# Seven quarter products in place of eight in differential attention's queries and keys and in a recurrent block's key and value halves

## The reference, cut

```python
def diff_attention(x, w_qkv, w_o, lam, subln_g, lambda_init):
    q, k, v = jnp.split(x @ w_qkv, 3, axis=-1)
    ...
    s = jnp.einsum('bqhcd,bkhd->bhcqk', q_blk, k) * scale
    p = jax.nn.softmax(jnp.where(causal, s, -jnp.inf), axis=-1)
    attn = p[:, :, 0] - lam_full * p[:, :, 1]
    ...
def rwkv7_time_mix(x, mu, w_rkv, ...):
    xx = jnp.pad(x, ((0, 0), (1, 0), (0, 0)))[:, :-1] - x
    xm = x[None] + xx[None] * mu[:, None, None, :]
    r, k, v = jnp.einsum('nbsd,nde->nbse', xm[:3], w_rkv)
    ...
```

## Time and profile before

| | us |
|---|---|
| median of 3 runs | 1956.05 (1954.45 to 1958.23) |
| profiled execution | 1958.03 |
| its span | 1956.2 |
| TensorE busy | 1647.6 (84% of the span) |
| VectorE busy | 679.4 (35%) |
| ScalarE busy | 370.8 (19%) |
| GpSimd busy | 195.0 (10%) |
| chain that ended last | TensorE 59%, transfers 32%, VectorE 5% |
| mean granted clock of TensorE | 0.93 |

### The profile page before, as it was taken

How to read it: one execution, slowest core, us unless ns; L and a number is a source line. 1 busy time by engine, 2 the same in 40 slices (tenths; PEclk the granted TensorE clock), 3 DMA queues, 4 the chain that set the end, 5 groups by cost and what they waited for, 6 DMA issues and landing times.

```text
span 1956.2 us, 29793 instructions
## 1 busy us (share of the span) xinstructions
PE 1647.6 (84%) x12826; PEld 1038.9 (53%) x12826; DVE 679.4 (35%) x1163; ACT 370.8 (19%) x748; POOL 195.0 (10%) x91
## 2 busy tenths in 40 slices
PE   9999999999999998776666797999988778676664
PEld 7998986997995854222122242867954223221211
DVE  1564431464541265211111124573365211111103
ACT  1444101343211251000000011331211000000001
POOL 2331422331330000000000000000300000000000
PEclk9999999999999999978887998999999989987877
DMA  9341444251355438999999998222156999999994
GB/s 384 103 169 52 186 181 164 85 167 72 151 204 204 172 135 351 427 427 428 427 427 427 425 419 341 106 86 67 68 238 285 426 428 426 426 426 427 427 427 194
DMA packets 48228, 537.10 MB, mean 275 GB/s; under 512 B 4533, under 2 KB 12981, under 8 KB 15033
## 3 DMA queue, kind: packets, MB, share of 16 engines
q1 hardware_dynamic: 46752, 528.27, 65.9%
q10 hardware_dynamic: 1304, 6.51, 0.8%
HBM read 533.71 MB, written 1.05 MB: 273 GB/s over the span
## 4 chain that ended last, share of the span: by engine, by line
PE 59%; DMA 32%; DVE 5%; ACT 2%; issue 1%; POOL 0%; ACTq 0%; DVEq 0%
PE ps L450 48%; DMA extra<-in_moe_w_gu 12%; DMA arena<-in_moe_w_gu 9%; PE ps L462 8%; DMA arena<-in_moe_w_down 6%; DMA ring<-in_moe_w_gu 4%; PE ps L468 2%; DVE x L1545 1%; DVE arena L1534 1%; ACT arena L2459 1%; ACT arena L2455 1%; DVE arena L1539 1%; DVE arena L1545 0%; ACT L2455 0%; DMA tcom<-in_tcom 0%
## 5 line engine op out<-in xcount | busy, mean ns | idle before, releaser
L462 PE MATMUL ps<-arena 128*32 128x512 f32 (+1 forms) x1348 | 204.4, 689 | 81.3 <-DMA arena<-in_moe_w_gu 65.0
L450 PE MATMUL ps<-hT,ring 128*128 128x256 f32 (+1 forms) x1472 | 262.5, 336 | 0.0
L2459 ACT ACTIVATE arena<-ps 128x512 f32<-128x512 f32 (+4 forms) x150 | 90.2, 601 | 879.0 <-PE ps L462 493.3
L462 PE MATMUL ps<-ring,arena 128*32 128x512 f32 x1248 | 181.9, 715 | 88.5 <-DMA ring<-in_moe_w_gu 69.7
L450 PEld LDWEIGHTS ps<-hT,ring 128*128 128x128 f32 x1472 | 233.4, 191 | 25.6 <-issue 2.1
L1534 DVE TENSOR_TENSOR arena<-arena,ps 128x256 f32<-128x256 f32 (+3 forms) x119 | 64.5, 542 | 511.6 <-ACT arena L2455 433.7
L462 PEld LDWEIGHTS ps<-arena 128*32 128x32 f32 (+1 forms) x1348 | 48.9, 126 | 220.2 <-DMA arena<-in_moe_w_gu 97.5
L450 PE MATMUL ps<-arena 64*64 64x64 f32 (+11 forms) x1456 | 142.4, 344 | 26.3 <-ACT arena L2748 22.3
L450 PE MATMUL ps<-arena,ring 64*64 64x64 f32 (+3 forms) x1344 | 146.9, 292 | 3.1 <-ACT hT L2459 1.4
L462 PEld LDWEIGHTS ps<-ring,arena 128*32 128x32 f32 x1248 | 38.0, 121 | 207.0 <-DMA ring<-in_moe_w_gu 101.1
L450 PEld LDWEIGHTS ps<-arena,ring 64*64 64x64 f32 (+2 forms) x1344 | 129.1, 161 | 18.3 <-DVE arena L1545 1.8
(11 more groups left out here) (204 smaller groups left out, 1820.3 us busy)
## 6 DMA issues: line engine op xcount, KB each, us to landing
arena<-in_moe_w_gu SPq DMA_DIRECT2D x57, 2048.0 KB, 41.3
ring<-in_moe_w_gu SPq DMA_DIRECT2D x49, 2048.0 KB, 41.3
ring<-in_moe_w_down SPq DMA_DIRECT2D x35, 2048.0 KB, 41.3
arena<-in_moe_w_down SPq DMA_DIRECT2D x29, 2048.0 KB, 40.6
extra<-in_moe_w_gu SPq DMA_DIRECT2D x22, 2048.0 KB, 40.8
ring<-in_w_merge SPq DMA_DIRECT2D x16, 2048.0 KB, 8.2
ring<-in_w_in SPq DMA_DIRECT2D x9, 2048.0 KB, 7.3
ring<-in_attn_w_qkv SPq DMA_DIRECT2D x6, 2048.0 KB, 7.2
```

Of the source, the lines that this page charges most:

```text
L450: i = t.matmul(o, l, r, start=first, stop=last, skip_group_check=True)
L462: i = t.matmul(o, l, r, start=first, stop=last, skip_group_check=True)
L2459: s.activation(o, a, ACT.Copy).then_inc(*act.one(name))
```

## The change

The products q0, k0, q1, k1 of attention and k1 and v1 of the recurrent block are made from seven quarter products each. With the weight half cut in quarters a (by depth and columns) and the input in quarters b (by depth and tokens), the parts are p1 = a11 b11, p6 = s2 h2, p7 = a21' h3 and p5 = s1 h1 into one PSUM tile ("a"), and p2 = a12 b21, p4 = a22 h4 and p3 = s4 b22 into a second ("b"). Each part is 8 matmuls with 128 columns (v1: 4 matmuls with 256). GpSimd makes a21' = a11 - a21 in place, s2 = a22 - a21', s1 = a11 + s2 and, when p6 is done, s4 = a12 - s2 over s2; the four input sums h are made once for attention and once each for k1 and v1. ScalarE copies p1's quarter, VectorE adds the others: four additions after p5 ("half": tile a is free), one after p2 and two after p3 ("out").

Scores wait for VectorE's "out" in place of ScalarE's copy. In attention the parts of q1 and k1 stand between the units where the column groups stood. VectorE makes q1's first additions after u0, its last after u1, k1's first after u2, its last after u3. The ring's slots of these products come free with part 3.

The diff, cut to its core. TensorE in attention:

```diff
-        def proj_qk(name, half, *cs):
-            n = f"da {name}{half}"
-            p = opened(n, cs[0] == 0, cs[-1] == 3, (act, n))
-            mm(proj_T(wcols(m.w(n), KT, 512), hT, KT, [(p[:, c * 256:(c + 1) * 256], slice(c * P, (c + 1) * P)) for c in cs]),
-               n if cs[-1] == 3 else None)
+        def proj_qk(name, half, *parts):
...
+                if q in (1, 2):
+                    tile(name2, *(((dve, n + " out"),) if late else ((act, n + " p1"), (dve, n + " half"))))
...
+                elif q == 6:
+                    t.wait_ge(*pool("da hsum"))
+                    t.wait_ge(*pool(n + " s2"))
+                elif q == 5:
+                    t.wait_ge(*pool(n + " s1"))
+                elif q == 3:
+                    t.wait_ge(*pool(n + " s4"))
+                mm([(p[:, 256 * i + P * e:256 * i + P * e + P], a[:, k, P * e:P * e + P], b[:, k, :], k == 0, k == 3)
+                    for e in range(2) for k in range(4)], f"{n} p{q}")
...
-            t.wait_ge(*act(f"da q{g // 2}"))
-            t.wait_ge(*act(f"da k{g // 2}"))
+            t.wait_ge(*dve(f"da q{g // 2} out"))
+            t.wait_ge(*dve(f"da k{g // 2} out"))
```

TensorE in the recurrent block (the inner `seven` gives out the parts 1, 6, 7, 5 and 2, 4, 3; ahead of 6 it waits for "hsum", ahead of 3 for "s4"):

```diff
-        proj("k", "rw mix1", r.xa, (1,))
+        seven("rw k1", r.xa, False)
...
+            if half:
+                seven(n, r.xc, True)
+                return
```

VectorE in attention; in the recurrent block it makes the same seven additions for "rw k1" ahead of `mix(0)` and for "rw v1" between `inverse_starts(0)` and `inverse_starts(1)`:

```diff
+        def first_sums(name, half):
...
+            v.wait_ge(*act(n + " p1"))
+            tt(c12, c11, area(p, 1), ADD)
+            v.wait_ge(*pe(n + " p5"))
+            tt(c21, c12, area(p, 2), ADD)
+            tt(c22, c21, area(p, 3), ADD)
+            tt(c12, c12, area(p, 3), ADD, n + " half")
+
+        def last_sums(name, half):
...
+            v.wait_ge(*pe(n + " p2"))
+            tt(c11, c11, area(p, 0), ADD)
+            v.wait_ge(*pe(n + " p3"))
+            tt(c21, c21, area(p, 2), ADD)
+            tt(c12, c12, area(p, 3), ADD, n + " out")
```

GpSimd in attention:

```diff
+    for c, name in enumerate(("q0", "k0", "q1", "k1")):
+        n, s2 = "da " + name, d.s2[c % 2]
+        (a11, a12), (a21, a22) = quarters(wcols(m.w(n), KT, 512))
+        g.wait_ge(*m.w.landed(n))
+        both(a21, a11, a21, SUB)
...
+        both(s2, a22, a21, SUB, n + " s2")
+        if c:
+            g.wait_ge(*pe("da " + ("q0", "k0", "q1")[c - 1] + " p5"))
+        both(s1, a11, s2, ADD, n + " s1")
...
+        g.wait_ge(*pe(n + " p6"))
+        both(s2, a12, s2, SUB, n + " s4")
```

GpSimd in the recurrent block:

```diff
+            for n, x, mixed, was in (("rw k1", m.rw.xa, "rw mix1", "moe0 end"), ("rw v1", m.rw.xc, "rw mix2", "rw k1 p3")):
...
+                g.wait_ge(*m.w.landed(n))
+                both(a21, a11, a21, SUB)
+                g.wait_ge(*pe(was))
+                both(s2, a22, a21, SUB)
+                both(s1, a11, s2, ADD)
+                g.wait_ge(*dve(mixed))
+                both(h3, b22, b12, SUB)
+                both(h1, b12, b11, SUB)
+                both(h2, b22, h1, SUB)
+                both(h4, b21, h2, SUB, n + " hsum")
+                g.wait_ge(*pe(n + " p6"))
+                both(s2, a12, s2, SUB, n + " s4")
```

More of the change, by code:

```diff
@@ L370, in memory @@
     d.S2, d.P2 = ([carve(512), carve(1024)] for _ in range(2))
+    d.hsum = [flat(m.mT)[:, 512 * i:512 * i + 512].rearrange("p (k s) -> p k s", k=4) for i in range(4)]
+    d.s2 = [carve(1024).rearrange("p (k n) -> p k n", k=4) for _ in range(2)]
+    at[0] = OWN - 1024
+    d.s1 = carve(1024).rearrange("p (k n) -> p k n", k=4)
     at[0] = 0
@@ L1257, in rwkv, with seven, part @@
                 for c in range(4)], "rw k0" if k == KT - 1 else None)
-        proj("k", "rw mix1", r.xa, (1,))
+        (h1, h2, h3, h4), (s1, s2) = m.hsum, m.wsum
+        def seven(n, x, turned):
+            (a11, a12), (a21, a22) = quarters(wcols(m.w(n), KT, 512))
+            (b11, b12), (b21, b22) = [[x[:, 4 * k:4 * k + 4, P * i:P * i + P] for i in range(NT)] for k in range(2)]
+            def part(p, i, a, b, q):
+                if turned:
+                    mm([(p[:, 256 * i:256 * i + 256], b[:, k, :], a[:, k, :], k == 0, k == 3) for k in range(4)], f"{n} p{q}")
+                else:
+                    mm([(p[:, 256 * i + P * c:256 * i + P * c + P], a[:, k, P * c:P * c + P], b[:, k, :], k == 0, k == 3)
+                        for c in range(2) for k in range(4)], f"{n} p{q}")
+            p = tile(n + " a", (act, n + " p1"), (dve, n + " half"))
+            t.wait_ge(*m.w.landed(n))
+            part(p, 0, a11, b11, 1)
+            t.wait_ge(*pool(n + " hsum"))
+            part(p, 1, s2, h2, 6)
+            part(p, 2, a21, h3, 7)
+            part(p, 3, s1, h1, 5)
+            p = tile(n + " b", (dve, n + " out"))
+            part(p, 0, a12, b21, 2)
+            part(p, 2, a22, h4, 4)
+            t.wait_ge(*pool(n + " s4"))
+            part(p, 3, s2, b22, 3)
+        seven("rw k1", r.xa, False)
         lv = wcols(m.w("rw lora1"), KT, 288)
@@ L1966, in oT_half @@
                MUL, None, n + " out b")
-        for n in range(4):
+        for name in "qk":
+            first_sums(name, 0)
+            last_sums(name, 0)
+        for n, more in enumerate((lambda: first_sums("q", 1), lambda: last_sums("q", 1), lambda: first_sums("k", 1), lambda: last_sums("k", 1))):
             front(*units[n])
             back(*units[n])
+            more()
         squares(1, 0)
@@ L2244, in rwkv, with seven @@
         mix(4, r.xc)
-        v.wait_ge(*pe("rw k1"))
+        def seven(n, c4):
+            (c11, c12), (c21, c22) = c4
+            p = ps(n + " a")
+            v.wait_ge(*act(n + " p1"))
+            tt(c12, c11, area_of(p, 1, c11), ADD)
+            v.wait_ge(*pe(n + " p5"))
+            tt(c21, c12, area_of(p, 2, c11), ADD)
+            tt(c22, c21, area_of(p, 3, c11), ADD)
+            tt(c12, c12, area_of(p, 3, c11), ADD, n + " half")
+            p = ps(n + " b")
+            v.wait_ge(*pe(n + " p2"))
+            tt(c11, c11, area_of(p, 0, c11), ADD)
+            v.wait_ge(*pe(n + " p3"))
+            tt(c21, c21, area_of(p, 2, c11), ADD)
+            tt(c12, c12, area_of(p, 3, c11), ADD, n + " out")
+        seven("rw k1", [[r.kT[:, 4 + 2 * j:6 + 2 * j, P * i:P * i + P] for i in range(NT)] for j in range(2)])
         mix(0, r.xa)
@@ L2332, in rwkv @@
             inverse_starts(i)
+            if i == 0:
+                seven("rw v1", [[r.vt[:, j, 512 + 256 * n:768 + 256 * n] for j in range(NT)] for n in range(2)])
         v.wait_ge(*pe("rw bonT"))
@@ L2871, in rwkv @@
                        bias=vcol(bias, 4 * half + c))
+        s.wait_ge(*dve("rw k1 out"))
         for k in range(KT):
@@ L2891, in rwkv @@
         s.wait_ge(*dve("rw pc"))
-        for half in range(2):
-            n = f"rw v{half}"
-            s.wait_ge(*pe(n))
-            cp(r.vt[:, :, 512 * half:512 * half + 512], ps(n).rearrange("p (t n) -> p t n", t=NT), n)
+        s.wait_ge(*pe("rw v0"))
+        cp(r.vt[:, :, 0:512], ps("rw v0").rearrange("p (t n) -> p t n", t=NT), "rw v0")
+        s.wait_ge(*pe("rw v1 p6"))
+        cp(r.vt[:, 0, 512:768], ps("rw v1 a")[:, 0:256], "rw v1 p1")
         def out(i, n, dst, mark=" out"):
```

73 lines of the change are left out of this document (56 added, 17 removed).

## The result

| | us |
|---|---|
| before, median of 7 runs | 1956.89 |
| after, median of 7 runs | 1963.96 (1960.01 to 1967.15) |
| ratio | 1.0038, interval 1.0028 to 1.0049 |
| after, once more (11 runs) | 1964.43, ratio 1.0034, interval 1.0019 to 1.0049 |
| forecast | 1962.5, range 1953 to 1968 |

The changed kernel is slower, by about 7 us. The profiled execution of after took 1967.15 with a span of 1965.1; it is the longest of its seven, so not all of its 9 us over the profile of before belong to the change. To keep chance apart I cut the span at four marks that every trace has: q0's first matmul, the issue of the next chunk into `extra` (765.00 in the earlier trace rows), the first transposes of the recurrent block, and the next issue into `extra` (1375.09 in the earlier trace rows). The stretches between them are called A (attention), M (the first experts) and R (the recurrent block).

The account below looks back on a forecast made before the run. TensorE's path in attention and the recurrent block was taken to set when expert-weight transfers start, and so the kernel's end. Attention +3.5 and recurrent block +3.0 gave +6.5 over the median 1956.05: 1962.5 us, range 1953 to 1968.

Parts of the forecast that it names:

- q0 and k0, -2.8: Attention's first two products: seven parts save 1.4 us of TensorE each, with GpSimd's sums and VectorE's additions costing nothing.
- The sums hold VectorE: GpSimd's sums and VectorE's two-input SBUF instructions wait for each other, as in the first layer; turn-taking given chance 0.58.
- taking turns, each waits for one sum: Attention, u0's two products: 2 x 2.43 plus 0.3 us, so the second ends at 671.25 in place of 666.09.
- Pauses in attention: TensorE idles 1.3 us ahead of the third score, 4.4 or 2.1 at u0's values, then 3.
- Attention +3.5: Differential attention: +2.7 us net of q0 and k0's gain, plus 0.8 for half clock; between +1.5 and +5.6.
- The second rival, no holding: GpSimd and VectorE don't hold each other: attention -3.6, in all -6.5 us, 1949.5; chance 0.17.
- the term for VectorE's additions: Second rival, attention: quarter adds of 1.85 us push u1 by 1.7, but TensorE has other parts to do meanwhile.
- k1, -0.8: Recurrent block: -1.4 us on TensorE, sums hold the first mix instructions about 1.2; net between -1.4 and +0.9.
- v1: Recurrent block: N0 idles 1.6 us, part 6 waits 3.0 for input sums until 1328.4; +2.9, up to +4.5.
- The mis-sized term: TensorE runs at half clock after a pause: 3.3 us so cost 1.65; v1 up to +4.5 with such a stretch.
- The sum: Whole kernel: attention +3.5 and recurrent block +3.0 make +6.5 us, 1962.5 against the median.
- A and R carry through to the end: Attention's end sets the expert transfers' start, likewise the recurrent block; each us won or lost reaches the kernel's end.

Follow-up runs that it names:

- the run with the sums cut short: Changed kernel with q1's fourth weight sum and all four of attention's k1 cut to one column; one execution, only attention read: A 135.59 us, against 139.15.
- the second trace of before: The kernel before, unchanged, profiled once more: A 136.62, M 453.15, R 157.64 us.
- the recurrent block alone: Seven parts in the recurrent block only, attention as in the kernel before: R 162.44 us, ratio 1.0023 to the kernel before, +4.5 us.
- v1 early: Changed kernel with v1's four input sums made before GpSimd waits for v1's weights: R 156.11 us, ratio 1.0011 to the kernel before, +2.2 us.
- q0 and k0 alone: Seven parts for q0 and k0 only, all else as in the kernel before: ratio 0.9983, 3.3 us faster than before.
- q0, k0, k1 and v1 early: Kernel before with seven parts for q0, k0 and the recurrent block's k1 and v1, v1's input sums made early: ratio 0.9997.
- the two runs of attention alone: Seven parts in attention only, recurrent block as in the kernel before, run twice: ratios 1.0045 (+8.8 us) and 1.0017 (+3.3 us).
- the needless matmuls: Changed kernel with eight needless matmuls between v1's part 1 and its wait for GpSimd: R 159.40 us, ratio 1.0036 to the kernel before.
- GpSimd's order: Changed kernel with attention k1's first two weight sums ahead of q1's fourth, its third behind u0's last product: A 139.43 us, ratio 1.0045 to the kernel before.
- q0, k0 and k1: Kernel before with seven parts for q0 and k0 in attention and k1 in the recurrent block: ratio 1.0008, +1.6 us.

## Why the prediction held, step by step

- **q0 and k0, -2.8.** Right: -2.76 from the first part to the first score, and 3.3 us of time by themselves.
- **The sums hold VectorE.** Right in kind, 3.6 us by the run with the sums cut short. The step "taking turns, each waits for one sum" failed: u0's first product did not wait, its second ended 2.5 later and not 5.2. The next to go is the one that asked first. A slip of the working is in it too: a first product that finds 0.3 of a running sum left waits 0.3, and only the second a whole sum, which is 2.7 by turns as well. The holds of the small instructions at 658.36, 0.50, and 666.62, 1.06, were not in the working.
- **Pauses in attention.** The values of u0 waited 1.50 (2.1 to 4.4 forecast), the fourth score 2.79 (3), the third score not at all (1.3). The 1.37 ahead of u1's values was missed: ScalarE does u2's exponentials, and waits for VectorE's u2, ahead of the copy that u1's values need.
- **Attention +3.5.** Right in kind, 1.1 too dear: measured +2.4 in A, inside +1.5 to +5.6, with a whole stretch at half clock of 3.4 us in it where half of one was taken.
- **The second rival, no holding.** It gave -3.6 for attention. Without holding the stretch from the first score to the fifth is +1.5, so with q0 and k0 -1.3: the term for VectorE's additions, taken as hidden by TensorE's other parts, was too small by 2.3, of which up to 1.7 is clock (3.4 us at half).
- **k1, -0.8.** N0 came 99.92 behind the transposes in place of 101.23, both with 13.65 us at half clock at the start, 1.3 less: the mix instructions were not held in the changed kernel. (With 17.07 us at half clock the second trace of before has 102.84.) They were in the kernel with the recurrent block alone, by the 1.27 that was forecast as 1.2. Which it is depends on when the weights land against the end of the experts' stage.
- **v1.** Part 6 was put at 1328.4 on the axis of before; with the 2.05 by which v0 started later that is 1330.45, and it started at 1330.36. N0's wait of 1.6 did not come in the changed kernel, since VectorE's pair stayed together, and so the pause before part 6 was 4.27 in place of 3.0; in the recurrent block alone, where the pair was parted, N0 waited 0.96 and part 6 2.87, much as forecast. The mis-sized term is the clock: up to 1.65 allowed, half of it taken, 2.6 measured. So R is +4.6 to +5.2 in place of +3.0, at its upper bound of +5.
- **The sum.** +6.5 forecast, +7.1 to +7.4 in A + R, +7.4 (5.5 to 9.6) in time. Attention had been put 1.1 too dear and the recurrent block about 2 too cheap, and these partly cancelled: that the sum came within 1 us is in part luck.
- **A and R carry through to the end.** Borne out to 1 us by five of eleven: the changed kernel (A + R +7.4 and +7.1, time +7.4 and +6.7), the recurrent block alone (+4.9, +4.5), v1 early (+1.2, +2.2) and q0 and k0 alone (-2.8, -3.3). In the other six the time is longer than A + R say: by 1.3 for q0, k0, k1 and v1 early, 1.6 and 7.5 for the two runs of attention alone, 2.5 for the needless matmuls, 2.8 for GpSimd's order and 4.1 for q0, k0 and k1. A + R is from one trace and the time from many; M is the place where they may have lost it.

## What to carry to other kernels

In this kernel, work taken off TensorE and given to GpSimd as sums was free only where VectorE did not run the instructions that these sums hold (two inputs in SBUF, or small ones from SBUF to SBUF) at the same time and where the consumer had something else to do until the last sum was done: q0 and k0 met both conditions and gained 2.8 us up to the first score; q1 and k1 met neither and lost 5.1 between the first score and the fifth, v1 lost 5.5 between N0 and N1. Ahead of such a change, lay the new instructions of GpSimd beside VectorE's at the place, and count how long the longest chain of sums is from the moment its last input is there; inputs that are known earlier can be summed earlier. A pause of TensorE has a second price in the clock behind it: 2.6 us behind the pause of 4.27 ahead of part 6.

## What the runs showed of the hardware that I had not expected

- GpSimd's duration in the trace includes its wait for VectorE (4.42 and 4.22 for sums of 2.35), so a long sum is a sign of being held, not of work.
- Very small instructions of VectorE, 128x4 and 128x2 with one tensor input, are held as well (1.23 and 1.19 in place of 0.17, 1.43 in place of 0.17). Those on 128x4 stand at the head of ScalarE's exponentials, so holding them delays the unit as holding a large product does. Size isn't what decides: the reduction of 128x512 at 665.90 was not held.
- The scalar-tensor-tensor instruction of 128x256 beside GpSimd's input sums for k1 (1.37 to 1.59 in place of 0.48, four from 1234.27) and that of 128x2048 beside the weight sums (4.24 in place of 2.29) are held, while additions out of PSUM are not (1.85 for four beside a running sum).
- Needless matmuls in a pause kept the granted clock at 1.00 behind it and saved 2.6 us on the stretch.
